# Token-major projection products of 512 columns, two more upper parts in the weight ring, constants and masks after the first weight unit

## The chip, the core and the metric

The kernel runs on one core of one Trainium2 chip. The metric is device time in microseconds (us), the median of three runs. Before the change it is 1793.27 us (1791.59 to 1796.1).

## What is computed

Two layers of a hybrid backbone, for 128 context tokens and 256 latent tokens together (384 tokens, 3 tiles of 128), all in fp32 with D_MODEL = 1024. The change touches the first half of a layer, which is this part of the reference:

```python
h = rmsnorm(x, p['norms'][0]) * (1.0 + scale1) + shift1     # shift and scale from silu(c) @ ada_w
z = h @ p['w_in']                                           # (384 x 1024) @ (1024 x 7184)
qa, ka, va, ub, vb, qkvc, bc, ac, zc, gates = jnp.split(z, split_idx, axis=-1)
qa, ka = rmsnorm per head of 64, latent tokens with rope_2d
o_a = block_attention(qa, k_all, v_all)
o_b = chunk_gmlp(jax.nn.gelu(ub), jax.nn.gelu(vb), ...)
o_c, s_fin = deltanet_mixer(qkvc, bc, ac, zc, ...)          # short conv, silu, l2norm of q and k, chunked scan
g_a, g_b, g_c = jnp.split(jax.nn.sigmoid(gates), 3, axis=-1)
merged = g_a * (o_a @ wb[0]) + g_b * (o_b @ wb[1]) + g_c * (o_c @ wb[2])
x = x + gate1 * rmsnorm(merged @ p['w_out'], p['norms'][1])
```

Then comes a dense SwiGLU (layer 0) or eight experts with top 2 (layer 1).

## The kernel before, in words

**Split products.** An fp32 matrix is used as two parts: an upper one in TensorE's faster fp32 format, which ACT writes as a copy (`upper_w`), and a lower one, raw minus upper, which POOL or DVE writes over the raw data (`lower_block`). A product is three matmuls per k tile: h upper x w upper, h lower x w upper, h upper x w lower; there are 8 k tiles. Semaphore `w_up` counts ACT's upper blocks of 128 columns, `p_lo` and `v_lo` the lower blocks of POOL and of DVE. A block is 128 partitions x 1024.

**The units of w_in.** `WIN` cuts the matrix into 14 units of 512 columns (2 MB each, one DMA). Units 0 to 2 are q, k and v of the DeltaNet, computed feature-major: the weights stand still, 384 tokens stream (`feature_step`, 12 tiles with `proj_mm` 1 to 12); DVE runs the short convolution beside them (L2662). Then a small product BA (`T_BA` = 12) gives the decays and write strengths, which lie feature-major until they are turned (`T_BT` = 19). Five units are token-major, the activation standing still and the weights streaming (`token_tiles`, L1227): unit 3 the attention queries (`T_A` = 13), unit 4 keys and values (`T_A + 3`), units 5 and 6 the gMLP's u and v (`T_UV` = 20), and unit 13 the DeltaNet's Z (`T_Z` = 50). Units 7 to 12 are the gates, feature-major (`T_G` = 26).

**A token-major unit before.** `token_tiles` goes over two halves g of 256 columns, and inside over the three token tiles t: 2 x 3 x 8 x 3 = 144 matmuls of 256 columns (L1250 to L1252). Each half waits for its two lower blocks. Between the halves it signals `half_mm` and may insert other products.

**What is inserted.** `row_sums` (L1302) sums the squares of the DeltaNet's q and k over rows, with signal `dst`, between the halves of unit 4. ACT takes the square roots (L2122, `droot`), DVE the reciprocals (L2680, first `qkn`), and `spread` (L1319) spreads them on TensorE before and inside unit 5. `decay_sums` stands between the halves of unit 6. After unit 6 TensorE waits for `qkn` 9 and turns the DeltaNet's v and k (kvt): 24 transposes recorded at the helper's line L1134. After it come the gate units.

**Banks.** A product of a tile lies in one PSUM bank. `proj_mm` counts finished tiles, `proj_ev` those that ACT has copied out (`evac`, L2073). v of the gMLP is copied out through Gelu with a Square behind it (L2157). The turns of v and k use banks in which v's tiles lie: `qkn` and `proj_ev` gate them.

**The ring.** All weights come through a ring of four slots of 2 MB each, in the order of the list `order`. An entry is a raw unit ("w"), the upper parts of one ("w_hi"), or a column block of ada_w ("ada"), from which the modulation is computed between the tiles. Entry u uses slot u mod 4, and whoever writes it first waits until entry u - 4 was wholly used (`freed`). Upper parts of units 7 to 13 lie in the ring; those of units 0 to 6 lie in `granules` (w_gran in the trace), a buffer of four blocks. Its block m can be written again when the unit before has used it: ACT waits for `proj_mm` or, from unit 4 on, for `half_mm`.

**Queues.** Each engine runs its own list in order. SP issues the ring's DMAs (L834, `load`), each waiting for its slot, and parks x (`xpark`, `parked` when it has landed). POOL issues small loads: biases, router, caches, masks. POOL makes the lower parts of units 1 to 3, DVE those of 4 to 6 and of the gates. The square `asq` of attention's q and k goes through ACT (L2131). The constants `cst` (997 columns x 128 partitions: identity, triangular masks, ones, rope tables, selectors) are loaded by the first DMA of SP's queue; the masks of the chunked scan (768 columns) by POOL after ring entry 0 has landed, and DVE casts them (signal `bf_ok`).

## Time and profile before

| | |
|---|---|
| median of three runs | 1793.27 us (1791.59 to 1796.1) |
| profiled execution, its time / its span | 1790.62 us / 1788.8 us |
| PE, matmuls | 1727.8 us busy, 97%, x13909 |
| PEld, weight loads | 1451.5 us, 81% |
| DVE | 1030.6 us, 58% |
| ACT | 799.1 us, 45% |
| POOL | 262.6 us, 15% |
| chain that ended last | PE 81%, DMA 7%, DVE 5%, ACT 3%, issue 3%, POOL 1% |
| granted TensorE clock, mean | 0.998 |
| DMA | 351.27 MB, mean 196 GB/s |

The span is the time from the first to the last recorded instruction of the profiled execution; its own time has some 2 us around it. The chain says for each stretch what the end had to wait for: 81% of it is matmuls. Where one engine is that full, the places to read are those at which it stands still, and what the engine in front of it is doing there. In the rows, "x24" is a count of instructions in one piece of time; a bracket "[4.43 <-ACT ...]" says how long the engine was idle before it and who released it; times are from the start of the span. A matmul's busy time overlaps that of the next one, so pitches are read from starts.

### The profile page before, as it was taken

To read this page: it belongs to the slowest core of one execution; us is meant where nothing else is said; L and a number is where in the kernel's file an instruction comes from. 1 tells how busy PE (TensorE), PEld (TensorE's weight loads), DVE (VectorE), ACT (ScalarE), POOL (GpSimd) and SP (SyncE) were. 2 spreads that over 40 slices of the span, in tenths; PEclk is the share of its full clock that TensorE was granted. 3 is DMA by queue.
4 is the path that set the end of the run, shared out by engine and by line. 5 is a ranking of instruction groups with operands and counts; after the bars stand their busy time and mean duration, and the time that the engine had idled before them with its cause. 6 is when DMAs were issued, how large, how long until landed. Compare 5 with 4: busy or idle time off the path is not lost.

```text
span 1788.8 us, 32059 instructions
## 1 busy us (share of the span) xinstructions
PE 1727.8 (97%) x13909; PEld 1451.5 (81%) x13909; DVE 1030.6 (58%) x1383; ACT 799.1 (45%) x1114; POOL 262.6 (15%) x228
## 2 busy tenths in 40 slices
PE   5999999999999999999999999999999999999997
PEld 4889788989979999888899788899878555556885
DVE  2867655547635344336965745556658443436987
ACT  3356733235434223225366523246356433336775
POOL 2620042240000000004500214230002000000001
PEclk9999999999999999999999999999999999999999
DMA  9661152216741443347541323137468989989994
GB/s 360 205 245 67 48 225 74 94 49 205 266 162 63 141 137 98 141 157 265 199 167 54 138 102 106 48 119 256 184 224 317 349 304 332 319 279 393 392 380 188
DMA packets 175189, 351.27 MB, mean 196 GB/s; under 512 B 5161, under 2 KB 60481, under 8 KB 174544
## 3 DMA queue, kind: packets, MB, share of 16 engines
q1 hardware_dynamic: 170880, 334.50, 52.2%
q0 software_dynamic: 4176, 14.82, 2.3%
q8 instruction: 105, 1.72, 0.4%
q14 instruction: 28, 0.23, 0.0%
HBM read 320.46 MB, written 28.84 MB: 195 GB/s over the span
## 4 chain that ended last, share of the span: by engine, by line
PE 81%; DMA 7%; DVE 5%; ACT 3%; issue 3%; POOL 1%; SPq 0%; POOLq 0%; DVEq 0%; ACTq 0%
PE bank L1210 6%; PE bank L1827 6%; PE bank L1212 5%; PE bank L1211 5%; PE bank L1687 3%; PE bank L1689 3%; PE bank L1688 3%; PE bank L1250 3%; PE bank L1803 3%; PE bank L1252 3%; PE bank L1251 3%; PE bank L1806 3%; PE bank L1804 3%; PE bank L1134 2%; PE bank L1739 2%
## 5 line engine op out<-in xcount | busy, mean ns | idle before, releaser
L1986 ACT ACTIVATE ring_split<-ring 128x1024 fp32r<-128x1024 f32 (+2 forms) x84 | 119.2, 1444 | 174.5 <-DMA ring<-in_ffn_w_up 103.9
L1212 PE MATMUL bank<-hT_hi,ring_split 128*128 128x384 f32 x576 | 193.4, 336 | 0.0
L2928 DVE TENSOR_TENSOR ring_split<-ring,ring_split 128x2048 fp32r<-128x2048 f32 (+1 forms) x28 | 73.8, 2670 | 138.7 <-ACT ring_split L1986 138.7
L1210 PE MATMUL bank<-hT_hi,ring_split 128*128 128x384 f32 x384 | 140.8, 367 | 0.7 <-issue 0.7
L1252 PE MATMUL bank<-ring_split,hT_hi 128*128 128x256 f32 x480 | 135.2, 282 | 0.0
L807 DVE TENSOR_TENSOR ring_split<-ring,w_upper_a 128x2048 fp32r<-128x2048 f32 (+2 forms) x54 | 96.5, 1814 | 62.0 <-PE bank L1827 42.3
L1211 PE MATMUL bank<-hT_lo,ring_split 128*128 128x384 f32 x384 | 128.3, 334 | 0.0
L1687 PE MATMUL bank<-hT_hi,ring_split 128*128 128x384 f32 x352 | 119.1, 338 | 0.0
L1689 PE MATMUL bank<-hT_hi,ring_split 128*128 128x384 f32 x352 | 118.6, 337 | 0.0
L1688 PE MATMUL bank<-hT_lo,ring_split 128*128 128x384 f32 x352 | 117.2, 333 | 0.0
L1250 PE MATMUL bank<-w_gran,hT_hi 128*128 128x256 f32 x384 | 107.7, 280 | 1.3 <-ACT ktok L1986 1.3
L1212 PEld LDWEIGHTS bank<-hT_hi,ring_split 128*128 128x128 f32 x576 | 108.1, 188 | 0.0
L1251 PE MATMUL bank<-w_gran,hT_lo 128*128 128x256 f32 x384 | 107.9, 281 | 0.0
L802 ACT ACTIVATE w_upper_a<-ring 128x2048 fp32r<-128x2048 f32 (+2 forms) x54 | 80.5, 1529 | 60.2 <-PE bank L1806 31.2
L1986 ACT ACTIVATE work<-bank 128x256 f32<-128x256 f32 (+2 forms) x111 | 45.1, 437 | 136.1 <-PE bank L1492 54.8
L1827 PE MATMUL bank<-ring,hT 128*64 128x512 f32 (+1 forms) x452 | 101.4, 572 | 2.9 <-ACT hT L1986 1.7
L2662 DVE SCALAR_TENSOR_TENSOR conv<-gates,rowsT,conv 128x388 f32<-128x388 f32 x96 | 100.7, 1049 | 3.4
L807 DVE TENSOR_TENSOR ring_split<-ring,w_upper_b 128x2048 fp32r<-128x2048 f32 (+2 forms) x48 | 84.8, 1797 | 16.7 <-ACT w_upper_b L802 10.8
L2073 ACT ACTIVATE gates<-bank 128x384 f32<-128x384 f32 (+1 forms) x60 | 30.8, 513 | 138.2 <-PE bank L1212 124.9
L1252 PEld LDWEIGHTS bank<-ring_split,hT_hi 128*128 128x128 f32 x480 | 90.2, 188 | 0.0
L1804 PE MATMUL bank<-ring_split,xg_hi 128*128 128x512 f32 (+1 forms) x240 | 88.8, 370 | 0.0
L802 ACT ACTIVATE w_upper_b<-ring 128x2048 fp32r<-128x2048 f32 (+2 forms) x48 | 71.0, 1516 | 30.0 <-PE bank L1806 24.7
(468 smaller groups left out, 4348.0 us busy)
## 6 DMA issues: line engine op xcount, KB each, us to landing
ring<-in_w_in SPq DMA_DIRECT2D x28, 2048.0 KB, 8.9
ring<-in_ada_w SPq DMA_DIRECT2D x24, 2048.0 KB, 8.7
ring<-in_moe_w_down SPq DMA_DIRECT2D x18, 1536.0 KB, 7.6
ring<-in_moe_w_gate SPq DMA_DIRECT2D x26, 1024.0 KB, 7.3
ring<-in_moe_w_up SPq DMA_DIRECT2D x26, 1024.0 KB, 9.8
ring<-in_w_branch SPq DMA_DIRECT2D x8, 1536.0 KB, 7.2
ring<-in_ffn_w_gate SPq DMA_DIRECT2D x11, 1024.0 KB, 5.3
ring<-in_ffn_w_up SPq DMA_DIRECT2D x11, 1024.0 KB, 7.8
```

Source lines behind the costliest of these rows:

```text
L807: op.tensor_tensor(m_half(m_place(j, visit_of(i), True), j, h), m_half(m_place(j, visit_of(i)), j, h), m_half(w_upper[j % 2], j, h).bitcas ...
L1210: mm(out, hi, hT_hi[:, k], start=k == 0, stop=False)
L1211: mm(out, hi, hT_lo[:, k], start=False, stop=False)
L1212: last = mm(out, lo, hT_hi[:, k], start=False, stop=k == KT - 1)
L1250: mm(out, hT_hi[:, k, ts], hi[k], start=k == 0, stop=False)
L1251: mm(out, hT_lo[:, k, ts], hi[k], start=False, stop=False)
L1252: last = mm(out, hT_hi[:, k, ts], lo[:, k], start=False, stop=k == KT - 1)
L1687: mm(out, w_hi(k), x_hi[:, k], start=k == 0, stop=False)
L1688: mm(out, w_hi(k), x_lo[:, k], start=False, stop=False)
L1689: last = mm(out, w_lo(k), x_hi[:, k], start=False, stop=k == n - 1)
L1827: last = mm(out[CH[y], :, 0:w], x[:, kt], part, start=kt == 0, stop=kt == n_k - 1)
L1986: return go(out, in_, ACT.Copy)
```

## The change

1. `token_tiles` makes products of 512 columns, over whole tiles, for units 4, 5 and 6 and for tiles 1 and 2 of units 3 and 13; the first tile of those two stays in halves. A block of `granules` or of the ring is read as four blocks of 128 columns. The inserted products come after tile 1 (`row_sums`, `decay_sums`) and after tiles 0 and 1 (`spread`).
2. `RING_HI`: the upper parts of units 4 and 6 lie in the ring. It has two more entries per layer, so all that follow move one or two slots on.
3. POOL makes the lower parts of units 4 and 6, DVE those of 5 and the gates.
4. ACT writes all four upper blocks of unit 4 before it waits for `parked`, those of 5 before it takes out tile 0 of keys and values and the square roots, those of 6 behind the copy of BA; `half_mm` goes.
5. The first DMA carries 149 columns of the constants. The other 848 follow the first weight unit on SP's queue; the masks come on POOL's queue behind the router's load, into another buffer. DVE casts them after the convolution; ACT waits for them before `asq`; TensorE waits for the second part before BA.

The order of columns in `cst` and the slices that name them change with it.

```diff
-           w_up=57, p_lo=20, v_lo=37, half_mm=4)
+           w_up=57, p_lo=28, v_lo=29)
...
+NEARLY = P + 2 + 3 + NE + ADA_W
...
+        RING_HI = (4, 6, 7, 8, 9, 10, 11, 12, 13)
...
-                order += [(kind, layer, i) for i in range(first, last) for kind in (("w", "w_hi") if 7 <= i < 14 else ("w",))]
+                order += [(kind, layer, i) for i in range(first, last) for kind in (("w", "w_hi") if i in RING_HI else ("w",))]
...
-            if i < 7:
+            if i not in RING_HI:
                 return granules[:, m]
...
+        LO_VECTOR = (5, 7, 8, 9, 10, 11, 12)
...
-            sp.dma_start(cst[:, :], cst_d[:, 0:NRES]).then_inc(cst_in, 16)
+            sp.dma_start(cst[:, 0:NEARLY], cst_d[:, 0:NEARLY]).then_inc(cst_in, 16)
...
+                        if layer == 0 and i == 0:
+                            sp.dma_start(cst[:, NEARLY:NRES], cst_d[:, NEARLY:NRES]).then_inc(cst_in, 16)
...
-            pool.wait_ge(s_slot[slot(0)], full(0))
-            pool.dma_start(RX[:, 6144:6144 + NMASK], cst_d[:, NRES:NRES + NMASK]).then_inc(mask_in, 16)
...
+                if layer == 0:
+                    pool.dma_start(OT[:, 0:NMASK], cst_d[:, NRES:NRES + NMASK]).then_inc(mask_in, 16)
...
-                for q in range(4, 16):
-                    lower_block(q // 4, q % 4)
+                for i in (1, 2, 3, 4, 6):
+                    for m in range(4):
+                        lower_block(i, m)
...
-            def token_tiles(layer, n, i, between=None, after=()):
-
-                for g in range(2):
-                    wait(pe, "v_lo" if 4 <= i < 7 else "p_lo", layer, lo_n(i, 2 * g + 1) + 1)
...
-                    for t in range(NT):
...
-                        out = B[token_bank(n + t)][:, 256 * g:256 * (g + 1)]
...
-                    if g == 0 and i < 7:
-                        last.then_inc(S["half_mm"], 1)
-                    if g == 0 and between:
-                        between()
+            def token_tiles(layer, n, i, halves=False, after=()):
...
+                for t in range(NT):
...
+                    ts = slice(t * P, (t + 1) * P)
+                    for g0, g1 in ((0, 2), (2, 4)) if halves and t == 0 else ((0, 4),):
+                        if t == 0:
+                            wait(pe, "v_lo" if i in LO_VECTOR else "p_lo", layer, lo_n(i, g1 - 1) + 1)
+                        out, cs = B[token_bank(n + t)][:, P * g0:P * g1], slice(P * g0, P * g1)
                         for k in range(KT):
-                            mm(out, hT_hi[:, k, ts], hi[k], start=k == 0, stop=False)
...
+                            mm(out, hT_hi[:, k, ts], hi[:, g0:g1, k], start=k == 0, stop=False)
+                            mm(out, hT_lo[:, k, ts], hi[:, g0:g1, k], start=False, stop=False)
+                            last = mm(out, hT_hi[:, k, ts], lo[:, k, cs], start=False, stop=k == KT - 1)
+                    last.then_inc(S["proj_mm"], 1)
+                    for step in [x for at, x in after if at == t]:
+                        step()
...
+                pe.wait_ge(cst_in, 32)
                 bank_free(layer, T_BA)
...
-                token_tiles(layer, T_A, 3)
+                token_tiles(layer, T_A, 3, True)
...
-                token_tiles(layer, T_A + 3, 4, row_sums)
+                token_tiles(layer, T_A + 3, 4, False, ((1, row_sums),))
...
-                token_tiles(layer, T_UV, 5, None, (((0, 0), lambda: spread((3, 4, 5))), ((1, 0), lambda: spread((6, 7)))))
+                token_tiles(layer, T_UV, 5, False, ((0, lambda: spread((3, 4, 5))), (1, lambda: spread((6, 7)))))
...
-                token_tiles(layer, T_UV + 3, 6, decay_sums)
+                token_tiles(layer, T_UV + 3, 6, False, ((1, decay_sums),))
...
-                token_tiles(layer, T_Z, 13)
+                token_tiles(layer, T_Z, 13, True)
...
-                    if i >= 7:
+                    if i in RING_HI:
                         freed(act, at_ring("w_hi", layer, i))
...
-                elif 16 <= q < 28 and m < 2:
-                    wait(act, "half_mm", layer, i - 3)
-                elif 16 <= q < 28:
-                    wait(act, "proj_mm", layer, (T_A + 3, T_A + 6, T_UV + 3)[i - 4])
+                elif i == 5 and m == 0:
+                    wait(act, "proj_mm", layer, T_A + 3)
...
-                    act.wait_ge(bf_ok, 1)
...
+                for m in range(4):
+                    upper_w(layer, 4, m)
                 act.wait_ge(parked, 16 * (layer + 1))
-                for m in range(2):
-                    upper_w(layer, 4, m)
...
-                    if t == 2:
-                        upper_w(layer, 4, 2)
-                        upper_w(layer, 4, 3)
...
-                for m in range(2):
+                for m in range(4):
                     upper_w(layer, 5, m)
+                evac(T_A + 3, qkv[:, 0, 512:1024])
                 wait(act, "dst", layer, 1)
...
-                for m in range(2, 4):
-                    upper_w(layer, 5, m)
+                for m in range(4):
+                    upper_w(layer, 6, m)
                 wait(act, "proj_ev", layer, T_BT + 1)
+                act.wait_ge(bf_ok, 1)
                 go(asq, qkv[:, :, 0:768], ACT.Square).then_inc(S["a_sq"], 1)
...
-                for m in range(2):
-                    upper_w(layer, 6, m)
                 for t in range(NT):
                     evac(T_UV + t, uB[:, t], ACT.Gelu_apprx_tanh)
-                for m in range(2, 4):
-                    upper_w(layer, 6, m)
                 upper_w(layer, 7, 0)
...
-                    dve.wait_ge(mask_in, 16)
-                    v.tensor_copy(lmask[:, :], RX[:, 6144:6144 + NMASK]).then_inc(bf_ok, 1)
                     ada_take(ADA_FIRST, 0)
...
+                if layer == 0:
+                    dve.wait_ge(cst_in, 32)
+                    dve.wait_ge(mask_in, 16)
+                    v.tensor_copy(lmask[:, :], OT[:, 0:NMASK]).then_inc(bf_ok, 1)
...
-                for q in range(16, 22):
-                    lower_block(q // 4, q % 4)
+                for m in range(4):
+                    lower_block(5, m)
...
-                lower_block(5, 2)
-                lower_block(5, 3)
...
-                lower_block(6, 0)
-                lower_block(6, 1)
...
-                lower_block(6, 2)
-                lower_block(6, 3)
```

**SP's queue**, around the second half of the first layer's units 3 to 6: `ring` is the ring, `xpark` the parked x. Before:

```order
L847 DMA xpark<-work 128x3072 [waits xt_p]
L834 DMA ring<-in_w_in 128x8x512 [waits proj_mm]
L834 DMA ring<-in_w_in 128x8x512 [waits ada_mm]
L834 DMA ring<-in_w_in 128x8x512 [waits proj_mm]
L834 DMA ring<-in_ada_w 128x8x512 [waits ada_mm]
L834 DMA ring<-in_w_in 128x8x512 [waits proj_mm] x2
```

After:

```order
L850 DMA xpark<-work 128x3072 [waits xt_p]
L837 DMA ring<-in_w_in 128x8x512 [waits proj_mm] x2
L837 DMA ring<-in_w_in 128x8x512 [waits ada_mm]
L837 DMA ring<-in_ada_w 128x8x512 [waits proj_mm]
L837 DMA ring<-in_w_in 128x8x512 [waits proj_mm] x2
```

Behind `xpark` these are, in both, units 4, 5 and 6, an ada block, and units 7 and 8. Raw unit 5 followed an ada block in its slot and now follows unit 3, for whose end it waits; unit 6 followed unit 3 and now follows an ada block; the ada block takes the slot of unit 4's upper parts.

**ACT's queue**, around the square roots between units 4 and 5 (L2122 and L2120 are their table load, L2118 and L2115 the square before). Before:

```order
L1986 ACTIVATE w_gran<-ring 128x1024 [waits proj_mm] x2
L2116 ACTIVATE conv<-conv 128x1552 [waits conv]
L2118 ACTIVATE gates<-conv 128x3104 [waits silu]
L1986 ACTIVATE w_gran<-ring 128x1024 [waits half_mm,slot0_full]
L1986 ACTIVATE w_gran<-ring 128x1024 [waits half_mm]
L2122 ACT_TABLE_LOAD
L2122 ACTIVATE gates<-bank,cst 128x388 [waits dst]
L2123 ACTIVATE gates<-bank,cst 128x388
L2073 ACTIVATE work<-bank 128x512 [waits proj_mm] x3
L1986 ACTIVATE small<-bank 128x48 [waits proj_mm]
L1986 ACTIVATE w_gran<-ring 128x1024 [waits proj_mm] x2
```

After:

```order
L2113 ACTIVATE conv<-conv 128x1552 [waits conv]
L2115 ACTIVATE gates<-conv 128x3104 [waits silu]
L1989 ACTIVATE w_gran<-ring 128x1024 [waits proj_mm,slot1_full]
L1989 ACTIVATE w_gran<-ring 128x1024 x3
L2074 ACTIVATE work<-bank 128x512 [waits proj_mm]
L2120 ACT_TABLE_LOAD
L2120 ACTIVATE gates<-bank,cst 128x388 [waits dst]
L2121 ACTIVATE gates<-bank,cst 128x388
L2074 ACTIVATE work<-bank 128x512 [waits proj_mm] x2
L1989 ACTIVATE small<-bank 128x48 [waits proj_mm]
L1989 ACTIVATE ring_split<-ring 128x8x128 [waits proj_mm,slot2_full]
L1989 ACTIVATE ring_split<-ring 128x8x128 x3
```

Four copies of unit 5 and one evacuation stand ahead of the roots now, before there were two copies.

**ACT's queue**, around the copy of unit 7's first upper block (`ring_split`, in the ring), the exponentials of the decays (`small`) and the evacuations of v (`gates<-bank` behind `qkn`, with L2157 or L2152). Before:

```order
L1986 ACTIVATE w_gran<-ring 128x1024 [waits half_mm,slot1_full]
L1986 ACTIVATE w_gran<-ring 128x1024 [waits half_mm]
L2073 ACT_TABLE_LOAD
L2073 ACTIVATE gates<-bank 128x512 [waits proj_mm] x3
L1986 ACTIVATE w_gran<-ring 128x1024 [waits proj_mm] x2
L1986 ACTIVATE ring_split<-ring 128x8x128 [waits proj_mm,slot3_full]
L2150 ACT_TABLE_LOAD
L2150 ACTIVATE small<-small 128x24 [waits gc_v]
L2151 ACTIVATE small<-small 128x48
L2152 ACTIVATE small<-small 128x24
L2073 ACT_TABLE_LOAD [waits proj_mm]
L2073 ACTIVATE gates<-bank 128x512 [waits qkn]
```

After:

```order
L2074 ACT_TABLE_LOAD
L2074 ACTIVATE gates<-bank 128x512 [waits proj_mm] x3
L1989 ACTIVATE ring_split<-ring 128x8x128 [waits proj_mm,slot1_full]
L2145 ACT_TABLE_LOAD
L2145 ACTIVATE small<-small 128x24 [waits gc_v]
L2146 ACTIVATE small<-small 128x48
L2147 ACTIVATE small<-small 128x24
L2074 ACT_TABLE_LOAD [waits proj_mm]
L2074 ACTIVATE gates<-bank 128x512 [waits qkn]
```

The rows read alike, but the count of `proj_mm` for which the copy into the ring waits is another: before the slot was that of raw unit 5 (free at tile T_UV + 3), now it is that of raw unit 6 (T_UV + 6, the last tile of v).

## Rows read from the trace of the kernel before

**Rows 1.** Timeline, TensorE, 104.5 to 127 us (start us, us, engine, line, op, count, [idle <-releaser])
```profile
105.93 0.36 PE L1250 MATMUL bank<-w_gran,hT_hi 128*128 128x256 f32 x1 [0.66 <-ACT ktok L1986]
...
114.84 0.28 PE L1250 MATMUL bank<-w_gran,hT_hi 128*128 128x256 f32 x1
...
126.86 0.28 PE L1250 MATMUL bank<-w_gran,hT_hi 128*128 128x256 f32 x1
```
**Rows 2.** Timeline, TensorE, 764 to 775 us, in the FFN
```profile
764.11 0.39 PE L1737 MATMUL bank<-ring_split,hid_hi 128*128 128x512 f32 x1
...
774.99 0.39 PE L1737 MATMUL bank<-ring_split,hid_hi 128*128 128x512 f32 x1
```
**Rows 3.** Timeline, TensorE, 1290 to 1300 us, output projection of layer 1
```profile
1295.48 0.39 PE L1664 MATMUL bank<-wo_hi_c,merged_hi 128*128 128x512 f32 x1
...
1299.69 0.39 PE L1664 MATMUL bank<-wo_hi_c,merged_hi 128*128 128x512 f32 x1
```
**Rows 4.** Chain of waits, 0 to 70 us; windows: busy PE, PEld, DVE, ACT, POOL, PEclk, DMA share, GB/s
```profile
11.04 22.15 DMA ring<-in_ada_w
...
20.00:25.00 5.00, 5.00 (x40) 2.87 (x43) 0.56 (x1) 0.00 (x0) 0.00 (x0) 1.00 1.05 388
```
**Rows 5.** Timeline of SP's queue, 95 to 135 us; DMA issues (us to landing), 108 to 165
```profile
101.71 1.00 SPq L834 DMA_DIRECT2D ring<-in_w_in  x2
...
123.16 0.37 SPq L834 DMA_DIRECT2D ring<-in_w_in  x1
...
ring<-in_w_in SPq DMA_DIRECT2D x1, 2048.0 KB, 9.1
...
ring<-in_w_in SPq DMA_DIRECT2D x1, 2048.0 KB, 7.6
```
**Rows 6.** Timeline, ACT, 112 to 198 us
```profile
127.20 2.80 ACT L2118 ACTIVATE gates<-conv 128x3104 f32<-128x3104 f32 x1
...
133.73 1.28 ACT L2122 ACT_TABLE_LOAD   x1
135.03 0.58 ACT L2122 ACTIVATE gates<-bank,cst 128x388 f32<-128x388 f32 x1
...
164.97 1.05 ACT L1986 ACTIVATE ring_split<-ring 128x1024 fp32r<-128x1024 f32 x1
```
**Rows 7.** Timeline, POOL; instructions of L2662 on DVE (duration ns min/median/max)
```profile
55.20 8.08 POOL L1030 TENSOR_TENSOR ring_split<-ring,w_gran 128x1024 fp32r<-128x1024 f32 x3
...
L2662 DVE SCALAR_TENSOR_TENSOR conv<-gates,rowsT,conv x96: 622/623/2809, 55.0 to 903.2; 128x388 f32<-128x388 f32 x96
```
**Rows 8.** Timeline, TensorE, 131 to 151 us; DVE, 112 to 198 us
```profile
131.54 1.51 PE L1302 MATMUL bank<-gates,cst 128*32 128x388 f32 x16
...
142.15 0.59 PE L1319 MATMUL bank<-gates,cst 32*128 32x388 f32 x2
...
136.12 5.00 DVE L2680 RECIPROCAL gates<-gates 128x776 f32<-128x776 f32 x1 [0.96 <-ACT gates L2123]
```
**Rows 9.** Timeline, TensorE, 172 to 200 us and 965 to 985 us
```profile
180.25 2.88 PE L1134 MATMUL bank<-cst,conv 128*128 128x128 f32 x24
...
967.96 2.88 PE L1134 MATMUL bank<-cst,conv 128*128 128x128 f32 x24
```
**Rows 10.** Timeline, ACT, 112 to 198 us
```profile
172.43 0.22 ACT L2150 ACTIVATE small<-small 128x24 f32<-128x24 f32 x1 [5.11 <-DVE small L2734]
...
176.13 0.60 ACT L2073 ACTIVATE gates<-bank 128x512 f32<-128x512 f32 x1
...
177.68 0.60 ACT L2073 ACTIVATE gates<-bank 128x512 f32<-128x512 f32 x1 [0.19 <-PE bank L1252]
...
180.51 0.60 ACT L2073 ACTIVATE gates<-bank 128x512 f32<-128x512 f32 x1 [1.48 <-PE bank L1252]
```
**Rows 11.** Timeline, TensorE, 515 to 546 us; windows, 530 to 541 us
```profile
537.27 3.76 PE L1193 MATMUL bank<-diag,work 128*128 128x128 f32 x18 [4.43 <-ACT hT L2031]
...
537.00:538.00 1.00, 0.72 (x3) 0.73 (x4) 0.19 (x1) 0.97 (x3) 0.00 (x0) 0.50 1.09 347
```

More of the change, by code:

```diff
@@ L146, in constants @@
     same = (i // CHUNK) == (j // CHUNK)
-    parts = [np.eye(P), (i >= j) & same, (i <= j) & same, same, np.ones((P, P))]
+    parts = [np.eye(P), np.stack([np.arange(P) < CHUNK, np.arange(P) >= CHUNK], 1), np.tile([EPS, DK * EPS, 1.0], (P, 1)),
+             np.tile(np.arange(NE), (P, 1)), np.arange(P)[:, None] % ADA_M == np.arange(ADA_W)[None, :],
+             (i >= j) & same, (i <= j) & same, same, np.ones((P, P))]
     quarter = HD // 4
@@ L156, in constants @@
     parts.append(rope.reshape(P, -1))
-    parts.append(np.stack([np.arange(P) < CHUNK, np.arange(P) >= CHUNK], 1))
-    parts.append(np.tile([EPS, DK * EPS, 1.0], (P, 1)))
-    parts.append(np.tile(np.arange(NE), (P, 1)))
-    parts.append((np.arange(P)[:, None] % ADA_M == np.arange(ADA_W)[None, :]))
     parts.append((np.arange(P)[:, None] % BA_W == np.arange(BA_W)[None, :]))
@@ L233, in build @@
         oT = OT[:, :].rearrange("p (b k n) -> p b k n", b=3, k=4)
-        ident, inclL, inclU, same, ones = (cst[:, i * P:(i + 1) * P] for i in range(5))
-        rope = cst[:, 640:768].rearrange("p (t f a q) -> p t f a q", t=2, f=2, a=2)
-        chsel = cst[:, 768:770]
-        eps1, eps128, one1 = (cst[:, 770 + i:771 + i] for i in range(3))
-        iota8 = cst[:, 773:773 + NE]
-        ada_sel = cst[:, 773 + NE:773 + NE + ADA_W]
-        c_eye = 773 + NE + ADA_W + BA_W
+        ident, chsel = cst[:, 0:P], cst[:, P:P + 2]
+        eps1, eps128, one1 = (cst[:, P + 2 + i:P + 3 + i] for i in range(3))
+        iota8 = cst[:, P + 5:P + 5 + NE]
+        ada_sel = cst[:, P + 5 + NE:NEARLY]
+        inclL, inclU, same, ones = (cst[:, NEARLY + i * P:NEARLY + (i + 1) * P] for i in range(4))
+        rope = cst[:, NEARLY + 4 * P:NEARLY + 5 * P].rearrange("p (t f a q) -> p t f a q", t=2, f=2, a=2)
+        c_eye = NEARLY + 5 * P + BA_W
         ba_sel = cst[0:2 * BA_W, c_eye - BA_W:c_eye]
@@ L618, in lo_n @@
             q = 4 * i + m
-            return 0 if q == 0 else q - 1 if q < 4 else q if q < 16 else q - 15 if q < 28 else q - 36 if i == 13 else q - 15
+            if i in LO_VECTOR or q == 0:
+                return 0 if q == 0 else q - 19 if i == 5 else q - 23
+            return q - 1 if q < 4 else q if q < 20 else q - 4 if i == 6 else q - 28
         def feature_bank(n):
@@ new lines, in token_tiles @@
+            def token_tiles(layer, n, i, halves=False, after=()):
+                s0 = slot(at_ring("w", layer, i)) * SLOT
+                lo = v3(ringS[:, s0:s0 + SLOT], KT)
+                if i in RING_HI:
+                    s0 = slot(at_ring("w_hi", layer, i)) * SLOT
+                    hi = v3(ringS[:, s0:s0 + SLOT], KT).rearrange("p k (g n) -> p g k n", g=4)
+                else:
+                    hi = granules
+                for t in range(NT):
+                    if T_A <= n < T_A + 3:
+                        wait(pe, "proj_ev", layer, T_A)
+                    elif n == T_Z and t == NT - 1:
+                        wait(pe, "s_or", layer, 6)
+                    elif n == T_UV and t == 0:
+                        wait(pe, "proj_ev", layer, T_UV)
+                    elif n < T_G:
+                        wait(pe, "proj_ev", layer, n + t - 2 if n < T_BT else n if t == 2 else n + t - 5)
+                    ts = slice(t * P, (t + 1) * P)
[3 more added lines that the diff above has]
+                        out, cs = B[token_bank(n + t)][:, P * g0:P * g1], slice(P * g0, P * g1)
+                        for k in range(KT):
+                            mm(out, hT_hi[:, k, ts], hi[:, g0:g1, k], start=k == 0, stop=False)
[4 more added lines that the diff above has]
+                        step()
@@ L1354, in gate_steps @@
                         if k == 0:
-                            wait(pe, "v_lo", layer, 13 + n + 1)
+                            wait(pe, "v_lo", layer, lo_n(7 + n // 4, n % 4) + 1)
                             bank_free(layer, T_G + n)
@@ L2043, in upper_w @@
                     act.wait_ge(s_slot[slot(at_ring("w", layer, i))], full(at_ring("w", layer, i)))
-                    if i >= 7:
+                    if i in RING_HI:
                         freed(act, at_ring("w_hi", layer, i))
@@ L2123, in _ @@
                 go(dsq[:, 1], B[3][:, 0:COUT], ACT.Sqrt, bias=eps1).then_inc(S["droot"], 1)
-                for t in range(NT):
+                for t in range(1, NT):
                     evac(T_A + 3 + t, qkv[:, t, 512:1024])
```

22 lines of the change are left out of this document (removed).

## Prediction

> **What bounds the kernel now.** I read the busy times first (the table above: TensorE hardly ever rests), then the order of time around the five token-major units, engine by engine, and last the chain of waits at the start. Where TensorE never rests, a shorter stream of products pays directly, and every new wait of TensorE costs in full. The 256-column products come 34 triples in (126.86 - 114.84) us, 117.8 ns apart [rows 1]. Products of 512 columns run 16 triples in (774.99 - 764.11) us, 226.7 ns apart, in the FFN [rows 2], and 6 triples in 4.21 us, 234 ns apart, in the output projection [rows 3]. Two halves thus cost 235.6 ns and a whole 226.7 ns: 8.9 ns a pair, at worst 1.6. I take 8.9: that is the longer and steadier stretch, and it too streams split weights against a split activation.
>
> **The stream.** A unit is 8 k x 3 products x 3 tiles = 72 pairs; units 3 and 13 keep the first tile in halves, so they join 48. Per layer 48 + 3 x 72 + 48 = 312, in two layers 624. That is 624 x 8.9 ns = **-5.5 us** (at worst -1.0), of which 2 x 48 x 8.9 ns = -0.9 us is Z's.
> The Trainium skill ("TensorE: Matmul & The Clock Gate", Back-to-back issue gap) gives a fixed 2.5 ns above the columns per isolated product. By that the 624 saved starts would be worth only 1.6 us; the rows show 11 ns over the columns at 256.
>
> **The start.** The chain waits 22.15 us for the ada_w units and DMA moves 388 GB/s meanwhile [rows 4], so bytes ahead are time. Of the first constants transfer of 997 columns, 512 bytes each over the partitions, 149 columns stay, 848 columns (434,176 bytes) go behind the first weight unit, and the masks, 768 columns or 393,216 bytes, go behind it on POOL's queue. Both loaded before that unit landed. 827,392 bytes / 388 GB/s = **-2.1 us** (bounds 0 and -2.1). The rest of the constants now stands before unit 1 on SP's queue, +1.1 us for a unit that is needed only at the fifth feature tile; the mask transfer delays three cache loads used after 170 us; the cast of the masks moves on DVE to the end of the convolution, and ACT needs it only at the squares of q and k. I cost these at nothing; without that cover the unit's 1.1 us would show.
>
> **The waits of the first layer.** Times here are those of the trace, without the 2.1 us.
> *Unit 4.* Its raw unit is issued at 101.71 and lands, alone now, 7.6 us later [rows 5], at about 109.4. ACT's four copies take 1.05 us each [rows 6]. POOL does the lower parts now: three took 8.08 us [rows 7], so four take 10.8, from 110.5 to 121.3. Unit 3 starts at 105.9 [rows 1] and ends at 105.9 + 48 x 0.1178 + 48 x 0.2267 = 122.4, so no wait, with 1.1 us to spare.
> *Unit 5.* Here is the first. Unit 4's upper parts hold a ring slot, so raw unit 5 is loaded only when unit 3 is done, at 122.7; before it had landed long ago. Issued with unit 6 behind it, as unit 6 was with an ada unit at 123.16, it takes the 9.1 us of that one [rows 5]: 131.8. Four copies: 136.0. The key evacuation that now stands there 0.6, the table load 1.3, the two square roots 1.1 [rows 6]: 139.0. The reciprocal 5.0 [rows 8]: 144.0. TensorE comes to that point at 105.9 + 16.5 + 16.3 for units 3 and 4 + 1.5 for the row sums [rows 8] + 1.0 of issue gaps and small products = 141.2 and waits 2.8 us. Before it passed at 142.15 [rows 8]. Unit 5 so starts 1.8 us late, and units 5 and 6 give 144 x 8.9 ns = 1.3 back: unit 6 ends at 180.8 instead of 180.25 [rows 9].
> *The copy of unit 7.* This is the main term. ACT's first copy of unit 7's upper part writes into the next slot of the ring. Before that slot was unit 5's, free long ago: the copy ran at 164.97 [rows 6]. With two more places in the ring the slot is that of **unit 6, and the copy waits until unit 6 is wholly used**. It stands in ACT's queue ahead of the three decay exponentials and of the three evacuations of v. Behind it TensorE may turn only two banks before it needs all of v in SBUF. After the end of unit 6 ACT now does: start 0.26, copy 1.05, table load 1.3, three exponentials of 0.22 that overlap 0.5, table load 1.3, two tiles of v with their squares at 177.68 - 176.13 = 1.55 each, and the last evacuation 0.6 [rows 6, 10]: 8.1 us. Before the last evacuation ended 0.9 us after the unit (180.51 + 0.60), under the two banks of turns. So TensorE stands 8.1 - 0.9 = 7.2 us longer. Nothing after it makes this good: ACT's root of v, kvt copies and turns start as late, and before they ran hidden under TensorE's 24 turns, ada quads and gate products; they stay hidden.
> *The clock.* After 4.43 us of idling the granted clock was 0.50 from 537 on, and 18 turns took 3.76 us [rows 11], 0.209 each against 2.88 / 24 = 0.12 [rows 9]. The 16 turns behind the new stall cost 16 x 0.09 = 1.4 us more (bounds 0 and 3.76 - 18 x 0.12 = 1.6); I take 1.4, as this gap is longer than that one.
> Layer 0: +0.5 + 7.2 + 1.4 = **+9.1 us** (unit gains within).
>
> **The second layer.** It runs the same order 787.7 us later: the turns at 967.96 against 180.25 [rows 9]. But there unit 5 follows an ada unit in its slot and comes early. On the first layer's scale ACT's squares ended at 127.20 + 2.80 = 130.0 [rows 6]; two copies of unit 4 (2.1) leave the stretch before them and unit 3 ends 0.5 earlier, so 127.4. Four copies, the evacuation and the table load end at 133.5. The row sums end at 122.4 + 0.2 + 10.9 + 1.5 = 135.0, the roots at 136.1, the reciprocal at 141.1, and TensorE comes at 141.2: no wait. Units 3 to 6 give 264 x 8.9 ns = 2.3 us. The copy of unit 7 waits as above. -2.3 + 7.2 + 1.4 = **+6.3 us**.
>
> **Sum.** -2.1 + 9.1 + 6.3 - 0.9 (Z) = +12.4 us. The profiled execution took 1790.6 us (its span is 1788.8), so 1803.0; the median of the three runs, 1793.3, lies 2.7 us above it, and carried onto it the sum gives **1805.7 us**. A measurement of this kernel can tell 0.3% (5.4 us) from no change.
>
> **The rivals.**
> *Only the products count (0.08).* If ACT's copy is not late, or its wait is hidden, what is left is -5.5 - 2.1 = -7.6 us: 1785.7, faster. For it: TensorE has hardly a gap here today and nothing is added to its stream. Against it: TensorE's queue is in order, and only two banks stand between the unit and the wait for v. It decides at 3.8 us of net wait a layer: ACT would have to be done 4.7 us after the unit, not 8.1.
> *Stalls absorbed (0.12).* Later waits could take up a delay, such as a transfer that is already late: that asks for 8.4 of the 12.4 us, +4.0, 1797.3. For it: the weights of the FFN and experts keep DMA full. Against it: each load is freed by TensorE's own progress and moves with it.
> *DVE and POOL in each other's way (0.20).* DVE's convolution products, normally 623 ns, took up to 2809 ns while POOL split [rows 7]. Eight more POOL splits a layer fall beside it. If POOL's four for unit 4 alternate with DVE, each loses one DVE product: 4 x (2.7 + 0.62) = 13.3, from 110.5 to 123.8, 1.4 us after unit 3's end; the wait before unit 5, 2.8 us, may also lower the clock, 1.6 more, and unit 5 may land 1 us later. Together +4: 1809.7, slower still.
> The Trainium skill ("SBUF - State Buffer", Who interferes with whom) says such a pair excludes each other for a whole instruction: the later one fully blocks. By that rule the 13.3 us above is the better value, and this rival's 1809.7 the time; the long convolution products agree, the splits' 8.08 us for three only partly.
> *The forecast (0.60)*, 1805.7, with 1801 to 1810 of its own: the start gives 0 to 2.1, the 512 pitch costs up to 4.5, the clock 0 to 3.2 in both layers, the landing 1.5 either way.
> The range that holds 8 in 10 is 1796 to 1814. Faster by over 0.3% 0.08, within 0.12, slower 0.80.
>
> **What would show it.** In the changed profile: products of 512 columns 227 ns apart; ada_w ready near 31 us; a TensorE wait of about 2.8 us before the spreads of unit 5 in the first layer and none in the second; in both a wait of about 7 us for ACT in the turns of v, behind a copy into the ring that starts at the end of unit 6, and half clock after it. If that copy starts well before the end of unit 6, or the turns run through, the forecast is wrong and the first rival holds.

## The result

The changed kernel takes 1803.99 us (1801.67 to 1807.09, four runs) against 1792.43 us before on the same chip: a ratio of 1.0055 (95% interval 1.0041 to 1.0069), 9.9 us slower at the ratio (the two medians differ by 11.6). The forecast was 1805.7 us. The profiled execution took 1803.43 us, 12.8 more than that of before; the sum had 12.4. The profile of the kernel before was a favourable one: its mean granted clock was 0.998, and in the 62 executions of that kernel beside the experiments it was 0.990 to 0.997.

| | before | after |
|---|---|---|
| profiled execution / its span, us | 1790.62 / 1788.8 | 1803.43 / 1801.6 |
| PE busy, instructions | 1727.8, x13909 | 1733.9, x13285 |
| POOL busy | 262.6 | 301.8 |
| chain: PE, ACT | 81%, 3% | 80%, 5% |
| granted TensorE clock, mean | 0.998 | 0.991 |

TensorE has 624 matmuls less and is still busy longer: part of its products ran at half the granted clock. In the timeline of TensorE after (start us, us, engine, line, operation, count, idle before) these are the marks of the first layer, the first product of unit 3, its first one of 512 columns, the row sums, the spreads, the turns of v and k, and the ada products behind them:

```profile
103.74 0.39 PE L1257 MATMUL bank<-w_gran,hT_hi 128*128 128x256 f32 x1 [0.57 <-ACT ktok L1989]
...
109.51 0.39 PE L1257 MATMUL bank<-w_gran,hT_hi 128*128 128x512 f32 x1
...
131.71 1.51 PE L1305 MATMUL bank<-gates,cst 128*32 128x388 f32 x16
...
140.52 0.93 PE L1322 MATMUL bank<-gates,cst 32*128 32x388 f32 x6 [0.78 <-DVE gates L2678]
...
177.71 1.04 PE L1140 MATMUL bank<-cst,conv 128*128 128x128 f32 x8
185.54 3.27 PE L1140 MATMUL bank<-cst,conv 128*128 128x128 f32 x16 [6.79 <-ACT gates L2074]
188.74 1.92 PE L1161 MATMUL bank<-ring,small 128*32 128x512 f32 x16
```

Unit 6 ends at 177.7, 2.5 us earlier than before [rows 9] (2.2 of them because unit 3 starts earlier), and the 24 turns that ran in one piece there are torn after 8 by a wait of 6.79 us for ACT. What ACT does in it, after:

```profile
177.97 1.06 ACT L1989 ACTIVATE ring_split<-ring 128x1024 fp32r<-128x1024 f32 x1 [16.92 <-PE bank L1259]
179.04 1.28 ACT L2145 ACT_TABLE_LOAD   x1
180.34 0.22 ACT L2145 ACTIVATE small<-small 128x24 f32<-128x24 f32 x1
...
180.82 1.28 ACT L2074 ACT_TABLE_LOAD   x1
182.12 0.60 ACT L2074 ACTIVATE gates<-bank 128x512 f32<-128x512 f32 x1
...
184.88 0.60 ACT L2074 ACTIVATE gates<-bank 128x512 f32<-128x512 f32 x1
```

The copy of unit 7's first upper block starts as unit 6 ends, after 16.92 us in which ACT did nothing; before it ran at 164.97 [rows 6]. Behind it come the table load, the exponentials, the other table load and three tiles of v. The last is out at 185.48 and TensorE goes on at 185.54. The second layer does the same, and windows (busy PE, PEld, DVE, ACT, POOL, then PEclk, DMA share, GB/s) show the clock:

```profile
979.29 3.68 PE L1140 MATMUL bank<-cst,conv 128*128 128x128 f32 x16 [6.79 <-ACT gates L2074]
...
180.00:184.00 4.00, 0.00 (x0) 0.00 (x0) 0.28 (x1) 3.90 (x9) 0.00 (x0) 0.68 1.04 400
184.00:188.00 4.00, 2.46 (x12) 2.47 (x13) 0.12 (x1) 3.88 (x9) 0.00 (x0) 0.50 0.26 95
```

Marks of TensorE against those of before, each difference a plain subtraction of starts (before, after), add up to the whole:

| stretch | before | after | difference |
|---|---|---|---|
| start to unit 3 | 105.93 | 103.74 | -2.2 |
| unit 3 to the ada products behind the turns, layer 0 | 77.13 | 85.00 | +7.9 |
| from there to unit 3 of layer 1 | 710.58 | 709.79 | -0.8 |
| the same in layer 1 | 77.12 | 84.37 | +7.3 |
| the rest of the span | 818.0 | 818.7 | +0.7 |

### The profile page after: what moved, and what is told of

It is laid out like the page before. It is cut to its first block, busy times and chain, and to the rows that moved or that the text cites. A ratio compares the mean times of both kernels' runs of the same rounds, so it can differ in the third digit from the quotient of the medians.

```text
span 1801.6 us, 30821 instructions
## 1 busy us (share of the span) xinstructions
PE 1733.9 (96%) x13285; PEld 1427.2 (79%) x13285; DVE 1030.2 (57%) x1367; ACT 798.8 (44%) x1114; POOL 301.8 (17%) x244
## 4 chain that ended last, share of the span: by engine, by line
PE 80%; DMA 6%; DVE 5%; ACT 5%; issue 3%; POOL 1%; SPq 0%; POOLq 0%; DVEq 0%; ACTq 0%
PE bank L1216 6%; PE bank L1830 6%; PE bank L1218 5%; PE bank L1217 5%; PE bank L1690 3%; PE bank L1692 3%; PE bank L1691 3%; PE bank L1806 3%; PE bank L1807 3%; PE bank L1809 3%; PE bank L1257 3%; PE bank L1258 3%; PE bank L1259 3%; PE bank L1140 2%; PE bank L1161 2%
## 5 line engine op out<-in xcount | busy, mean ns | idle before, releaser
L1989 ACT ACTIVATE ring_split<-ring 128x1024 fp32r<-128x1024 f32 (+2 forms) x100 | 134.7, 1378 | 216.3 <-DMA ring<-in_ffn_w_up 106.2
L2655 DVE SCALAR_TENSOR_TENSOR conv<-gates,rowsT,conv 128x388 f32<-128x388 f32 x96 | 114.8, 1196 | 3.4
L1218 PEld LDWEIGHTS bank<-hT_hi,ring_split 128*128 128x128 f32 x576 | 109.0, 189 | 0.0
L1259 PE MATMUL bank<-ring_split,hT_hi 128*128 128x512 f32 (+1 forms) x272 | 99.6, 366 | 0.0
L810 DVE TENSOR_TENSOR ring_split<-ring,w_upper_b 128x2048 fp32r<-128x2048 f32 (+2 forms) x48 | 84.8, 1797 | 16.7 <-ACT w_upper_b L805 10.8
L805 ACT ACTIVATE w_upper_b<-ring 128x2048 fp32r<-128x2048 f32 (+2 forms) x48 | 71.0, 1516 | 30.5 <-PE bank L1809 26.5
L1035 POOL TENSOR_TENSOR ring_split<-ring,w_gran 128x1024 fp32r<-128x1024 f32 x30 | 76.4, 2557 | 46.7 <-ACT w_gran L1989 46.7
L1216 PEld LDWEIGHTS bank<-hT_hi,ring_split 128*128 128x128 f32 x384 | 72.1, 188 | 12.4 <-issue 7.1
L1830 PEld LDWEIGHTS bank<-ring,hT 128*64 128x64 f32 x452 | 33.1, 136 | 59.1 <-issue 55.9
```

The costliest lines, as they stand in the source:

```text
L805: nc.scalar.activation(m_half(w_upper[j % 2], j, h), m_half(m_place(j, visit_of(i)), j, h), ACT.Copy).then_inc(mw_hi, 1)
L810: op.tensor_tensor(m_half(m_place(j, visit_of(i), True), j, h), m_half(m_place(j, visit_of(i)), j, h), m_half(w_upper[j % 2], j, h).bitcas ...
L1216: mm(out, hi, hT_hi[:, k], start=k == 0, stop=False)
L1218: last = mm(out, lo, hT_hi[:, k], start=False, stop=k == KT - 1)
L1259: last = mm(out, hT_hi[:, k, ts], lo[:, k, cs], start=False, stop=k == KT - 1)
L1830: last = mm(out[CH[y], :, 0:w], x[:, kt], part, start=kt == 0, stop=kt == n_k - 1)
```

## The experiments

The theory: **ACT's copy waits for unit 6 through its ring slot and holds up, in ACT's queue, the work that TensorE needs.** The rivals: the new order and width of the products make v late; DVE and POOL exclude each other; the clock.

**e1: the copy behind the evacuations of v.**

```diff
-                upper_w(layer, 7, 0)
                 wait(act, "gc_v", layer, 1)
...
                     link(go(gsc, vB[:, t], ACT.Square, accum_out=vss[:, t:t + 1]))
+                upper_w(layer, 7, 0)
```

> The changed kernel with one line moved: ACT's copy of unit 7's first upper block stands behind the three evacuations of v instead of ahead of the decay exponentials. Theory (the copy waits for the end of unit 6 and holds up everything behind it on ACT): the wait of 6.79 us in the turns of v goes in both layers, and the half clock behind it; unit 7 still comes in time. 2 x (6.79 + 16 turns x 0.09) = 16.5 us less, some 2 of them given back because two later waits were shortened by the delay: 1787 to 1789 us, a ratio to the kernel before of 0.997 to 0.998. Rival 1 (the 512-column order itself makes v's tiles late, or the gate products now wait for unit 7): a wait of over 3 us stays between unit 6 and the gate products, 1796 or more. Rival 2 (DVE and POOL exclude each other and that is what costs): hardly any change, 1803.

Measured: 1788.92 us (1785.48 to 1790.95), a ratio of 0.9971 (0.9960 to 0.9982): faster than both kernels. TensorE and then ACT in e1:

```profile
178.59 2.88 PE L1140 MATMUL bank<-cst,conv 128*128 128x128 f32 x24
181.40 1.92 PE L1161 MATMUL bank<-ring,small 128*32 128x512 f32 x16
183.53 1.70 PE L1140 MATMUL bank<-cst,work 128*128 128x128 f32 x13 [0.21 <-ACT conv L1989]
```

```profile
178.85 0.60 ACT L2074 ACTIVATE gates<-bank 128x512 f32<-128x512 f32 x1 [0.59 <-PE bank L1259]
...
180.23 1.06 ACT L1989 ACTIVATE ring_split<-ring 128x1024 fp32r<-128x1024 f32 x1
```

The turns run in one piece of 2.88 us. The copy comes at 180.23 and nobody waits for it; what is left is 0.21 us. One line was the loss.

**e2: the dose.** The copy stands behind the exponentials and ahead of v.

> The changed kernel with the same copy placed between the decay exponentials and the evacuations of v. A dose: the exponentials and their table load then run hidden under unit 6. Theory: the wait in the turns falls by just their time, 1.28 + 0.50 = 1.8 us, from 6.79 to 5.0 us in both layers; copy, Gelu table load and three tiles of v stay behind the end of unit 6. If only the three tiles of v counted, it would be 6.79 still; if the queue were not the cause, no change either.

```profile
186.10 3.68 PE L1140 MATMUL bank<-cst,conv 128*128 128x128 f32 x16 [5.01 <-ACT gates L2074]
...
981.14 3.68 PE L1140 MATMUL bank<-cst,conv 128*128 128x128 f32 x16 [5.01 <-ACT gates L2074]
```

5.01 us in both layers, as expected: 1.8 us of ACT's work moved ahead of the copy took 1.8 us from TensorE's wait. The one execution took 1803.79 us all the same, not some 3.6 less than the changed kernel. Its unit 3 started 2.5 us later (106.21 against 103.74), and from there on it was 2.1 us faster; half clock in other places took part of the rest, such as in the 24 turns behind the FFN's first wait (5.8 us against 5.1). From a single execution only the wait is to be read here.

**e3: the wait alone, in the kernel before.**

```diff
+                wait(act, "proj_mm", layer, T_UV + 6)
                 upper_w(layer, 7, 0)
```

> The kernel before with nothing but one wait added: ACT's copy of unit 7's first upper block waits for the last tile of unit 6, as the ring makes it wait in the changed kernel. Theory: the same stall appears there, 6.8 us in the turns of v in each layer with half clock behind it, 8.2 to 8.6 us a layer: 1807 to 1810 us, a ratio of 1.009. Rival (the stall belongs to the new order of products, of banks or of the ring): well under that, 1800 or less.

Measured: 1809.84 us, a ratio of 1.0103 (1.0081 to 1.0126), within the 1807 to 1810 us of the theory.

```profile
187.58 3.67 PE L1134 MATMUL bank<-cst,conv 128*128 128x128 f32 x16 [6.73 <-ACT gates L2073]
...
986.57 3.67 PE L1134 MATMUL bank<-cst,conv 128*128 128x128 f32 x16 [6.73 <-ACT gates L2073]
```

The stall is 6.73 us there, without any product of 512 columns and with the old ring. e1 shows that the loss goes when v no longer stands behind the wait, e3 that the wait alone is enough for it. New order, width, banks, and DVE with POOL are out as its cause.

**e4: the width alone.** e1 with all token-major products in halves:

```diff
-                    for g0, g1 in ((0, 2), (2, 4)) if halves and t == 0 else ((0, 4),):
+                    for g0, g1 in ((0, 2), (2, 4)):
```

> The first kernel of this call (copy behind v), with every product of the token-major units in two halves of 256 columns, tile by tile. It measures the width alone: 624 pairs in two layers. By the pitches in the changed kernel's trace (117.8 and 231.4 ns) a pair costs 4.2 ns more: 2.6 us slower than that kernel. By the pitch of the FFN on which the prediction was made (226.7 ns) it would be 5.5 us; by a fixed cost of 2.5 ns per product 1.6 us.

Measured: 1796.06 us, a ratio to the kernel before of 1.0017 (1.0002 to 1.0033); against e1's median 7.1 us more, where 2.6 was expected: a miss. The products themselves fit better. From unit 3 to the turns e1 takes 178.59 - 104.68 = 73.91 us and e4 182.07 - 105.98 = 76.09; of the 2.18 more 0.87 are a longer wait before the spreads (1.60 against 0.73), so 1.31 us for 264 pairs, 5.0 ns each, 3.1 us for 624. The rest lies elsewhere. First, e4 starts unit 3 1.3 us later. Second, the FFN's first h waits 4.34 us instead of 3.28. Third, there is idle time that the trace calls "issue". It stands here in the kernel before, in e1 and in e4:

```profile
248.41 0.27 PE L1484 MATMUL bank<-work 64*64 64x64 f32 x1 [1.98 <-issue]
...
1035.87 0.46 PE L1484 MATMUL bank<-work 64*64 64x64 f32 x15 [1.94 <-issue]
```

```profile
247.78 0.69 PE L1495 MATMUL bank<-work 64*64 64x64 f32 x32 [0.91 <-issue]
```

```profile
252.59 0.29 PE L1487 MATMUL bank<-work 64*64 64x64 f32 x2 [1.89 <-issue]
...
1042.31 0.46 PE L1487 MATMUL bank<-work 64*64 64x64 f32 x16 [1.98 <-issue]
```

The five kernels with 13,909 matmuls (before, e3, e4, e7, e10) stand still for 1.9 to 2.1 us in layer 0 and for 1.6 to 2.7 us in layer 1 (e4 adds 0.70 us at 1048.19), e1 with 13,285 for 0.91 us and 0.27. These pieces are more than the 7.7 us between the two spans; against them e1's granted clock was low for longer near 840 and near 1640 us.

**e6 and e8: more instructions.** Both are e1 with small products added where TensorE waits at the start (n = 8, n = 40):

```diff
                 if layer == 0:
+                    keep_warm(7, n)
                     pe.wait_ge(sc_ok, 1)
```

> e1 with 8 small products of the identity more, while TensorE waits at the start, so that its stream is 16 instructions longer there. It tests what else e4 cost: the kernels with 256-column products stand still 1.9 to 2.1 us for nothing the profile shows (issue) near 250 us, beside an instruction packet, in the 31st of 32 short products; the ones with 512 columns 0.6 to 0.9 us, one group later. Up to there they have 528 instructions less; packets are some 250 instructions each (5 packets for 1,248), and 528 is two of them and about 16. Theory: with 16 more the wait is back in the short products, 1.9 to 2.1 us. If it hangs on the products' width and not on the count of instructions: 0.9 us as in e1.

> e1 with 40 such products more, 80 instructions. Theory: the wait for a packet of instructions is what the last packet's instructions fell short of some 7.2 us (5.2 us of them and 2.0 of waiting before, 6.3 and 0.9 in e1); the boundary falls 80 instructions earlier than in e1, at the end of nine long products, and the 256 instructions before it took some 6.5 us: a wait of 0.6 to 0.8 us, right before the group of short products. By width alone: 0.9 us where it is in e1.

```profile
249.93 0.39 PE L1488 MATMUL bank<-work 64*64 64x64 f32 x10 [1.87 <-issue]
```

```profile
251.25 0.46 PE L1505 MATMUL bank<-work 64*64 64x64 f32 x16 [1.78 <-issue]
```

e6: 1.87 us, back among the short products (in the 23rd, not the 31st). Eight products at the start of the program brought back a wait 230 us later that e1 had halved: it hangs on the count of instructions, not on the width. e8 fell otherwise than expected: 1.78 us, in the 17th product of a group, not 0.6 to 0.8 ahead of it. So the place moves with the count, but the rule for its size (7.2 us less the time of the last 256 instructions) is refuted; the size stays open.

The place can be counted in the traces. Ahead of this wait stand 3,214 or 3,215 matmuls and weight loads in the changed kernel, e1, e2, e5, e6 and e9, 3,470 in e8, and 3,727 or 3,728 in the five kernels with 13,909 matmuls: steps of 256, within two. e6 has the same count as e1, so its 16 more instructions moved the wait 8 products earlier in the program.

**e5 and e9: the same lesson at other places of ACT's queue.** e5 is e1 with three moves:

```diff
+                    if layer and m == 1:
+                        taken(0)
...
-                evac(T_A + 3, qkv[:, 0, 512:1024])
                 wait(act, "dst", layer, 1)
...
                 go(dsq[:, 1], B[3][:, 0:COUT], ACT.Sqrt, bias=eps1).then_inc(S["droot"], 1)
+                evac(T_A + 3, qkv[:, 0, 512:1024])
...
-                    ff_upper(0, None, slice(0, 1))
...
-                    h_upper(layer, 1, between=lambda: ada_copy(at["nb"], 7, ada_buf))
+                    h_upper(layer, 1, between=lambda: (ada_copy(at["nb"], 7, ada_buf), ff_upper(0, None, slice(0, 1))))
```

(`taken` is the evacuation of a feature tile.)

> The kernel with the copy behind v (e1), with the same lesson applied at three more places of ACT's queue: the square roots ahead of the evacuation of keys and values; in layer 1 the evacuation of feature tile 0 behind the second upper block of unit 0 instead of behind the fourth and BA's; in layer 0 the first upper copy of the FFN, which waits for its load, behind the first h step instead of ahead of all. Theory: the waits of 0.73 us (before the spreads), 1.97 us (layer 1, second feature tile) and 3.28 us (FFN's h) become 0.15, 0.6 and 1.2 us, 4.0 us less, and the half clock behind the last two goes in part, 0 to 1.5 us: 1783.5 to 1785 against e1's 1788.9, a ratio to the kernel before of 0.9945. Rival (these waits are other engines': DVE's lower parts or the load itself): within 1 us of e1.

Measured: 1791.12 us, 0.9980 (0.9968 to 0.9992), not the 1783.5 to 1785 of the theory. Timeline of TensorE in e5:

```profile
536.40 0.94 PE L1199 MATMUL bank<-diag,work 128*128 128x128 f32 x6 [1.99 <-ACT hT L2034]
...
538.70 1.65 PE L1199 MATMUL bank<-diag,work 128*128 128x128 f32 x6 [1.36 <-DVE hT L2622]
...
841.92 0.41 PE L1216 MATMUL bank<-hT_hi,w_gran 128*128 128x384 f32 x1 [1.97 <-POOL ring_split L1035]
```

Two of three failed in the rival's way. In the second layer the wait is 1.97 us as before, but now POOL ends it: its lower part is as late as ACT's copies were. In the FFN 3.28 became 1.99 + 1.36, the second released by DVE. Only the wait before the spreads is gone. Why e5 is 2.2 us above e1 by the medians isn't settled; in its profile the clock was low for longer behind the FFN's waits (some 10 us) and near 200 us. The lesson holds where the engine moved is the only late one.

> e1 with only one of e5's three moves, the one whose wait went there (0.73 us before the spreads of unit 5): the square roots ahead of the evacuation of keys and values. Theory (e5's loss came from its other two moves, in the FFN's h steps and the second layer's first tile): the wait is 0.15 us or gone in layer 0 and nothing else changes: 0.6 us less than e1, 1788.3, a ratio to the kernel before of 0.9967. Rival (something in e5's loss was this move's): 1790 or more.

e9, timed: 1790.45 us, 0.9973 (0.9961 to 0.9985), the same as e1 by the intervals. Its wait is 0.34 us instead of 0.73, not the 0.15 expected, and 0.4 us can't be told in the time. The median lies above the 1790 us that the rival named, but theory and rival both lie within the interval, so e9 does not decide what made e5 slower.

**e7 and e10: the constants alone.** The kernel before with only the constants and masks of the change:

> The kernel before with the constants and masks of the changed kernel alone (149 columns first, the rest and the masks behind the first weight unit). Theory: 827,392 bytes less ahead of ada_w at 388 GB/s, all marks 2.1 us earlier from the first turn of the modulation on (33.2 to 31.1 us, unit 3 from 105.9 to 103.8), no new wait behind it: about 1791. Rival: the rest of the constants delays unit 1 or the caches, or DVE's cast holds up the lower parts of unit 4: part of it lost before unit 5.

> The kernel before with the constants and masks of the changed kernel alone, timed. The forecast had 2.1 us for it. The mark at the last turns of the first h stood at 40.1 us in its one look, at 41.3 and 40.9 in the two profiles with the old constants and at 39.2 to 41.0 in seven others with the new ones (mean of all eight 40.2): by these marks it is worth 0.9 us, a ratio of 0.9995; by bytes over the rate 2.1 us, a ratio of 0.9988.

e7's one execution took 1790.89 us, e10 1792.65 us, a ratio of 0.9994 (0.9981 to 1.0007). No new wait stands behind them in the traces. The interval holds 0.9988 (2.1 us) and no gain at all; the marks of the first h say 0.9. Unit 3 starts at 105.50 us in e7 and at 105.14 in e10, against 105.93 before; e7's theory had 103.8. So a gain isn't shown in the time, and by the marks it is under the 2.1 us.

The traces show why. These are the ada products that wait for the load at the start, in the kernel before, in e3 (old constants too) and in the changed kernel:

```profile
33.24 1.93 PE L1155 MATMUL bank<-ring,small 128*32 128x512 f32 x16 [1.72 <-DMA ring<-in_ada_w]
...
32.83 1.93 PE L1155 MATMUL bank<-ring,small 128*32 128x512 f32 x16 [0.47 <-DMA ring<-in_ada_w]
...
31.18 1.93 PE L1161 MATMUL bank<-ring,small 128*32 128x512 f32 x16
```

TensorE waits there for ada_w, 1.72 or 0.47 us, with the old constants, and in none of the ten profiles with the new ones. An earlier load can take away no more than this wait; after that TensorE's own products ahead of it set the mark, and the first of these ada products starts anywhere from 21.8 to 23.5 us.

## Why the prediction was right

- **The copy of unit 7** was the cause, by its place, its length and its number: expected 8.1 us of ACT from the end of unit 6 to v's last tile, measured 185.48 - 177.71 = 7.8; expected 7.2 us of waiting in each layer, measured 6.79 in both. Shown by e1, e2 and e3.
- **The clock behind it**: 16 turns in 3.27 us instead of 1.92, 1.35 us, expected 1.4.
- **The stream** is the term that was mis-sized. It was priced at 226.7 ns per product of 512 columns, the FFN's pitch. Measured is (131.71 - 109.51) / 96 = 231.3 ns, near the other row's 234. A pair saves 4.3 ns by the pitch and 5.0 by e1 and e4, not 8.9: 2.7 to 3.1 us instead of 5.5. The Trainium skill's fixed 2.5 ns ("TensorE: Matmul & The Clock Gate", Back-to-back issue gap), which it gives for an isolated product, made it 1.6 us and was the nearer end by the pitch; measured in this stream, a product of 256 columns has 11 ns over its columns and one of 512 has 18, so the gap is not fixed here.
- **Unit 4** brought no wait. POOL's four lower parts took 10.28 us (expected 10.8 alone, 13.3 in turns with DVE). The rival of DVE and POOL named a real thing at a wrong price. POOL's blocks for unit 4 in layer 0, those for unit 6 (which run after the convolution has ended, so that only four more blocks a layer fall beside it and not eight), and DVE's convolution products in layer 1:

```profile
108.51 10.28 POOL L1035 TENSOR_TENSOR ring_split<-ring,ring_split 128x1024 fp32r<-128x1024 f32 x4 [4.92 <-ACT ring_split L1989]
141.01 9.50 POOL L1035 TENSOR_TENSOR ring_split<-ring,ring_split 128x1024 fp32r<-128x1024 f32 x4 [22.22 <-ACT ring_split L1989]
...
896.43 8.64 DVE L2655 SCALAR_TENSOR_TENSOR conv<-gates,rowsT,conv 128x388 f32<-128x388 f32 x4
```

Beside the convolution POOL took 10.28 us instead of 9.50, and DVE 8.64 instead of the 2.60 that four such products take without POOL (at 104.38): nearly all of the hindrance fell on DVE. The 2.7 us in the rival's 4 x (2.7 + 0.62) had been read beside the convolution [rows 7] and held POOL's loss already; with POOL's own 2.37 it is 12.0. For this pair the rule of the Trainium skill ("SBUF — State Buffer", Who interferes with whom), by which the 13.3 us were the better value, is right that DVE is held up, but doesn't give POOL's time here; the run decides.
- **Unit 5** came late in the first layer and not in the second, as forecast, but its wait was 0.78 us, not 2.8. The unit was used from 128.67 on, 7.9 us after its issue at 120.79 rather than 9.1; four copies took 3.90 and not 4.2; TensorE itself came 0.6 later.
- **The start** was 2.1 us earlier in the two profiles (41.30 and 39.24), as forecast, but that agreement is luck: the same mark lies between 39.2 and 41.0 in the ten profiles of kernels with the new constants, and unit 3 starts at 103.7 to 106.3, 105.4 in the mean, against 105.9 and 105.5 with the old ones. The step that failed is "bytes ahead are time": only the wait for ada_w, 1.72 us or less, could go.
- **Absorbed stalls**: the FFN's first wait fell from 4.43 to 3.29 us. It looked as if the delay had been absorbed; but e1, without the delay, has 3.28 too, and e3, with it, 4.51. Nor does it go with the products of 512 columns: e4, without them, has 4.34, but e8, with them, has 4.74. TensorE in e8, then ACT in e1 and in e8:

```profile
539.72 5.77 PE L1199 MATMUL bank<-diag,work 128*128 128x128 f32 x24 [4.74 <-ACT hT L2035]
...
531.57 1.91 ACT L1989 ACTIVATE ring_split<-ring 128x2048 fp32r<-128x2048 f32 x1 [4.01 <-DMA ring<-in_ffn_w_up]
...
536.96 1.91 ACT L1990 ACTIVATE ring_split<-ring 128x2048 fp32r<-128x2048 f32 x1 [5.28 <-DMA ring<-in_ffn_w_up]
```

ACT's first copy for the FFN stands ahead of the h step and waits for its load, 4.01 us in e1, 5.28 in e8, 4.94 before and 3.98 after. What makes the load land earlier or later is open.

Put into the forecast's own sum: layer 0 had 9.1; less 2.0 for unit 5's wait, less 0.4 for the copy's, plus 1.1 for the smaller gain of 264 pairs, 7.8, measured 7.9. Layer 1 had 6.3; plus 1.1, less 0.4, plus 0.4 because its 16 turns took 3.68 us, 7.4, measured 7.3. The two last rows of the table came to -0.1 where the forecast had -0.9 for Z alone; in the first of them the issue wait near 250 us (0.64 instead of 1.98) and the FFN's wait gave 2.5 us, and a stretch at half clock behind an unchanged wait took 1.5 back (the 96 products after it 18.60 us instead of 17.09). In the second the issue waits near 1040 us gave 2.2 (0.47 instead of 1.94 + 0.73), and half clock took 3.0 behind an unchanged wait of 0.82 us and 1.6 near 1652. None of these was a term of the forecast. So the stall (2 x 6.79 = 13.6 us) and the clock behind it (1.35 + 1.76 = 3.1) were foreseen with their cause; that all the rest came to -3.9 us, where the forecast had -4.8, is partly luck.

## What to carry to other kernels

A buffer that moves in a ring changes the waits of every later user, even of those that the change doesn't touch. List who frees each slot after such a change, and for every wait that became later ask what stands behind the waiting instruction in its queue; here the cure is one line, and it turns 1.0055 into 0.9971. A copy that is needed last should stand last.

## What the runs showed of the hardware

**Idle time without a releaser moves with the number of instructions.** Waits of 1.8 to 2.1 us in TensorE's stream of short products came and went with 8 products added 230 us earlier (e6), and with the 528 instructions (weight loads and matmuls) that 264 wider products save ahead of that place. Its place near 250 us is a count of TensorE's instructions, in steps of 256, within two (3,215, 3,470 or 3,728 ahead of it). An instruction packet (the profile's kind of DMA packet of that name, 16 KB) lies beside each: in all twelve traces the wait near 250 us ends 2.2 to 2.5 us after such a packet starts. A variant's gain of a few us may be that.

**The granted clock fell also behind a wait of 0.82 us**, and not always. The same 0.82 us wait behind the turns stands in all kernels. In the kernel before the clock stays full after it. In e10, which has the same products there, it is half for most of 7 us, and the next mark comes 28.2 us later (195.13 to 223.28) instead of 25.1 (195.92 to 221.01). Windows of the kernel before and of e10:

```profile
196.00:200.00 4.00, 4.00 (x32) 3.18 (x32) 2.67 (x13) 2.00 (x11) 0.00 (x0) 1.00 0.01 2
200.00:204.00 4.00, 4.00 (x24) 2.33 (x26) 2.63 (x7) 2.28 (x11) 0.00 (x0) 1.00 0.00 0
```

```profile
196.00:200.00 4.00, 4.00 (x18) 3.35 (x18) 1.89 (x9) 1.08 (x5) 0.00 (x0) 0.52 0.00 0
200.00:204.00 4.00, 4.00 (x19) 1.99 (x17) 1.30 (x4) 1.08 (x5) 0.00 (x0) 0.63 0.00 0
```

That is 3 us between two executions with no other difference there. Over the twelve traces and both layers this stretch took 25.1 us 8 times, 26.5 to 26.7 us 11 times and 28.1 us 5 times, in kernels with the change and without. So small terms can't be read from one span; they are read between marks.
